# One trunk layer on one core: the attention loop in another order, and bias parts cut during the projection

## The chip, the cores and the metric

The kernel runs on one core of a Trainium2 chip. A core has a matrix engine (TensorE, PE in the profile), a vector engine (VectorE, DVE), an activation engine (ScalarE, ACT), a general engine (GpSimd, POOL) and a queue engine (SyncE, SP). Each takes its own instructions in order, and they meet at semaphores. The metric is the device time of one launch in microseconds, median of the runs; less is better.

## What is computed

One decoder layer over 512 tokens of width 1024, in float32. Only the attention and the first step of the expert part matter here:

```
sc = q k^T * scale + bias[bucket(distance)], masked
branch A (8 heads, 128-token window, sinks):  p = exp(sc - m) / (sum + exp(sink - m))
branch B (4 heads, two maps each, causal):    a = softmax(sc1) - lam * softmax(sc2)
o_a = p v;   o_b = rms_norm(a v) * (1 - lam_init)
y = sigmoid(gza) * (o_a @ w_out[:512]) + sigmoid(gzb) * (o_b @ w_out[512:])
...
gu = xb @ w_gate_up[e] + b_gate_up[e]       # 32 experts, each block
```

## The kernel before

**Stages.** The program runs one stage after another: the modulation rows, the projection with `w_in`, attention, the merge with router (`merge_*`), the experts, and the final sum. Matrices are held as a rounded high part and a low part and multiplied in three products. The weights `b_gate_up` (32 x 2048) are added to a sum of products by a matmul with a selection matrix; for that they are cut into three bfloat16 parts, 96 rows in all (`bparts`), in seven steps on DVE (`bias_parts(0)` to `bias_parts(6)`).

**Projection.** It has eight units of four output chunks; DVE also sums the rows of the modulation there (`ada`). For each half of a unit's weights ACT makes the high part (`split_high`, tile `whf`), DVE the low part (`split_low`, tile `wlf`), and PE multiplies. `whf` and `wlf` have two slots: PE works from one while the other is filled. ACT also copies each finished chunk out of PSUM (`evac_done`), in units 0 to 2 to `qk`, in units 3 to 7 to `nat`.

**Attention.** There are 24 units, six for each of four query tiles n of 128 tokens: two of branch A (four heads at a time), then four of branch B (one head with its two maps). For unit i:
- PE: `scores(i)` (L401 for A, L406 for B), `transposed(i)` (L420, L424: the weights p turned by matmuls with the identity), `values(i)` (L441, L449: the products with V), and once for each tile `outputs_transposed` (L457).
- DVE: `before(i)` (scale, bias, row maximum: L484 to L507) and `after(i)` (division by the sum, in B the difference of the maps: L517 to L529), once for each tile `sub_norm` (L553, L558), which between its two instructions waits for a power taken on POOL.
- ACT: `exps(i)` (L590, L593), `copies(i)` (L606, the turned weights from PSUM to SBUF, tile `pt`), then the output of A (L609, tile `ota`) or, after the last B head of a tile, the sums of squares (L615), and once for each tile L620.

Scores have two places in PSUM and four in SBUF (`s_sb`), `pt` has two. The turned weights have one place in PSUM. The order is written out by hand, with one loop on each engine: `AHEAD` is 3, so scores and exponentials run three units ahead of the products. `bias_parts` stand in DVE's loop at i = 8 to 14. POOL loads their source, `ball`, at the start of attention.

**Around it.** `merge_pe` begins with the output projection (L651) as soon as the last `outputs_transposed` is copied.

Of the kernel before, what the change touches and what calls it, by code (L numbers as in the profile page):

```python
# [96 lines left out]
def program(nc, ctx, x, c, rel_bias_table, w_ada, b_ada, g_mix_pre, g_mix_post, g_ffn_pre, g_ffn_post, w_in, w_out,  # L97
# [12 lines left out]
    h2_d = dram("h_ffn", (T, D), F32)  # L110
    slot_d = dram("slot_rows", (T * E, 2), I32)
# [23 lines left out]
    ball = at("ball", [96, 2 * D], F32, 52 * KB)  # L135
# [148 lines left out]
    def sem(name):  # L284
# [7 lines left out]
    oh_in, biasv_out, wide_out, toep_in, wo_in, ball_in, grow_in = map(  # L292
        sem, ("oh_in", "biasv_out", "wide_out", "toep_in", "wo_in", "ball_in", "grow_in"))
# [95 lines left out]

    def attention_pe(pe):  # L390
# [71 lines left out]
        for i in range(len(UNITS)):  # L462
            transposed(i)
            if i + AHEAD < len(UNITS):
                scores(i + AHEAD)
            values(i)
            if i >= 2 and UNITS[i - 2][0] == "B" and UNITS[i - 2][2] == H_B - 1:
                outputs_transposed(UNITS[i - 2][1])
        outputs_transposed(TC - 1)

    def attention_dve(dve):
# [60 lines left out]
        def bias_parts(n):  # L532


            if n == 0:
                dve.wait_ge(ball_in, 16 * 3)
                dve.wait_ge(latemod_ready, 3)
                nc.vector.tensor_scalar(ball[:, D:2 * D], ball[:, D:2 * D], 1.0, None, ALU.add).then_inc(bias_step, 1)
                dve.wait_ge(bias_step, 1)
                nc.vector.tensor_copy(bparts[:], ball[:]).then_inc(bias_step, 1)  # L540
                return

            cut, lo = ((False, 1), (False, 2), (True, 1), (True, 2), (False, 2), (True, 2))[n - 1]
            rows = slice(32 * lo, 32 * lo + 32)
            dve.wait_ge(bias_step, n + 1)
            if cut:
                nc.vector.tensor_copy(bparts[rows, :], ball[rows, :]).then_inc(bias_step, 1)
            else:
                nc.vector.tensor_tensor(ball[rows, :], ball[rows, :], bparts[rows, :], ALU.subtract).then_inc(bias_step, 1)

        def sub_norm(n):
            dve.wait_ge(osq_ready, H_B * (n + 1))
            nc.vector.tensor_scalar(sn[:, 1, :], sn[:, 0, :], 1.0 / (2 * DH), EPS_SUB, ALU.mult,  # L553
                                    ALU.add).then_inc(sn_ready, 1)
            dve.wait_ge(sn_ready, 2 * n + 2)
# [16 lines left out]
        for i in range(len(UNITS)):  # L572
# [4 lines left out]
            if i and UNITS[i - 1][0] == "B" and UNITS[i - 1][2] == H_B - 1:  # L577
                sub_norm(UNITS[i - 1][1])
            if 8 <= i < 8 + N_BIAS:
                bias_parts(i - 8)  # L580
# [1304 lines left out]
```

## Time and profile before

| | |
|---|---|
| median of 3 runs | 1775.54 us (1775.3 to 1778.35) |
| the profiled execution | 1777.53 us, its span 1775.7 us |
| PE busy | 1663.3 us, 94% of the span |
| DVE busy | 1377.4 us, 78% |
| ACT busy | 1097.6 us, 62% |
| mean granted clock of TensorE | 0.953 of full |

The span is what the profiler saw between the first and the last instruction; 1.8 us of the execution lie around it. The clock is a share of 2.4 GHz; in any stretch it is 1.0 or 0.5, and a number between is a mean. The shares are means over very different stages. Attention is the stretch from 249 to 369 us.

### The profile page before, as it was taken

What the parts mean: (1) busy time and instruction counts of PE and PEld (TensorE: products, weight loads), DVE (VectorE), ACT (ScalarE), POOL (GpSimd) and SP (SyncE); (2) the same over time, 40 slices, a digit from 0 to 9 for tenths busy, and PEclk for the clock granted to TensorE, in tenths of its full rate; (3) what the DMA queues carried; (4) which work ended last, traced back from release to release, by engine and by line L of the source; (5) the groups of instructions that cost most, each with busy time, mean ns of one, the idle gap of its engine ahead of it and who ended that gap; (6) DMA issues with size and microseconds to landing.
All of it is one profiled execution on the core that took longest, in us unless ns stands there. A gap on an engine that the chain in (4) does not pass through costs nothing.

```text
span 1775.7 us, 19642 instructions
## 1 busy us (share of the span) xinstructions
PE 1663.3 (94%) x7482; PEld 1299.8 (73%) x7482; DVE 1377.4 (78%) x1029; ACT 1097.6 (62%) x903; POOL 199.0 (11%) x154
## 2 busy tenths in 40 slices
PE   8999986688679999999999999999999999999994
PEld 3788864444368888888888888888888888888882
DVE  3544458825558888988898889988989898989894
ACT  2322235531447777777777777777777777777772
POOL 1200000021300001100110011001000100011112
PEclk9999997888579999999999999999999999999997
DMA  8765430022499999999999999999999999999964
GB/s 310 226 236 198 168 125 1 1 77 73 140 361 398 390 385 381 367 386 382 378 355 388 383 375 366 388 392 380 361 383 387 375 370 390 380 370 361 382 244 155
DMA packets 156502, 540.14 MB, mean 304 GB/s; under 512 B 13949, under 2 KB 15081, under 8 KB 156292
## 3 DMA queue, kind: packets, MB, share of 16 engines
q1 hardware_dynamic: 140880, 500.20, 74.0%
q0 software_dynamic: 13424, 34.47, 8.0%
q10 hardware_dynamic: 2100, 4.21, 0.7%
q8 instruction: 57, 0.93, 0.2%
q14 instruction: 41, 0.33, 0.0%
HBM read 522.54 MB, written 29.26 MB: 311 GB/s over the span
## 4 chain that ended last, share of the span: by engine, by line
PE 74%; DMA 2%; DVE 2%; ACT 1%; issue 1%; POOL 0%; POOLq 0%; SPq 0%; ACTq 0%; DVEq 0%
PE ps L1103 64%; PE ps L1077 4%; PE ps L651 4%; PE ps L1093 2%; PE ps L671 1%; DMA expert_sums<-yb,icur 0%; DMA xb<-h_ffn,stab 0%; DMA sums<-expert_sums 0%; PE ps L449 0%; PE ps L664 0%; ACT h2t L755 0%; DMA slot_rows<-rows,dest 0%; DVE y L831 0%; DVE yo L1364 0%; POOL slot_rows L931 0%
## 5 line engine op out<-in xcount | busy, mean ns | idle before, releaser
L1221 DVE TENSOR_TENSOR wl<-rawm,wh 128x2048 fp32r<-128x2048 f32 x420 | 946.7, 2286 | 147.6 <-ACT wh L1150 143.1
L1150 ACT ACTIVATE wh<-rawm 128x2048 fp32r<-128x2048 f32 x420 | 802.0, 1919 | 260.7 <-PE ps L1103 260.7
L1103 PE MATMUL ps<-wh,xh 128*128 128x512 f32 x1120 | 360.2, 403 | 3.5 <-DVE xl L1234 3.5
L1103 PE MATMUL ps<-wl,xh 128*128 128x512 f32 x1120 | 346.9, 391 | 0.0
L1103 PE MATMUL ps<-wh,xl 128*128 128x512 f32 x1120 | 346.2, 390 | 0.0
L1103 PEld LDWEIGHTS ps<-wh,xh 128*128 128x128 f32 x1120 | 211.3, 189 | 53.1 <-DVE xl L1234 4.9
L1103 PEld LDWEIGHTS ps<-wl,xh 128*128 128x128 f32 x1120 | 211.2, 189 | 44.8
L1103 PEld LDWEIGHTS ps<-wh,xl 128*128 128x128 f32 x1120 | 211.3, 189 | 44.5
L1103 PE MATMUL ps<-wh,ah 128*128 128x512 f32 x560 | 179.4, 401 | 2.5 <-DVE al L1238 2.5
L1103 PE MATMUL ps<-wl,ah 128*128 128x512 f32 x560 | 174.2, 392 | 0.0
L1103 PE MATMUL ps<-wh,al 128*128 128x512 f32 x560 | 173.1, 390 | 0.0
L1306 POOL DMA_INDIRECT expert_sums<-yb,stab x32 | 50.9, 1590 | 1009.0 <-ACT yb L1184 658.1
L1103 PEld LDWEIGHTS ps<-wh,al 128*128 128x128 f32 x560 | 105.6, 189 | 23.1
L1103 PEld LDWEIGHTS ps<-wl,ah 128*128 128x128 f32 x560 | 105.5, 188 | 22.7
L1103 PEld LDWEIGHTS ps<-wh,ah 128*128 128x128 f32 x560 | 100.3, 189 | 19.6 <-issue 3.0
L1745 DVE TENSOR_TENSOR wlf<-raw,whf 128x2048 fp32r<-128x2048 f32 (+1 forms) x18 | 39.1, 2173 | 90.1 <-ACT whf L1480 90.1
L1480 ACT ACTIVATE whf<-raw 128x2048 fp32r<-128x2048 f32 (+1 forms) x18 | 32.7, 1817 | 64.2 <-PE ps L1612 64.0
L1610 PE MATMUL ps<-whf,hh 128*128 128x512 f32 (+1 forms) x192 | 71.3, 372 | 0.0
L1612 PE MATMUL ps<-whf,hl 128*128 128x512 f32 (+1 forms) x192 | 71.1, 370 | 0.0
L1611 PE MATMUL ps<-wlf,hh 128*128 128x512 f32 (+1 forms) x192 | 71.0, 370 | 0.0
L1295 POOL DMA_INDIRECT xb<-h_ffn,stab x32 | 65.4, 2043 | 47.5 <-PE ps L1077 36.1
L1176 ACT ACTIVATE ah<-ps 128x1024 fp32r<-128x1024 f32 x35 | 35.9, 1026 | 55.3 <-PE ps L1103 55.3
(254 smaller groups left out, 1610.5 us busy)
## 6 DMA issues: line engine op xcount, KB each, us to landing
rawm<-in_w_gate_up SPq DMA_DIRECT2D x280, 1024.0 KB, 9.6
rawm<-in_w_down SPq DMA_DIRECT2D x140, 1024.0 KB, 7.8
raw<-in_w_ada SPq DMA_DIRECT2D x20, 1024.0 KB, 5.1
raw<-in_w_in SPq DMA_DIRECT2D x16, 1024.0 KB, 5.2
rawx<-in_w_ada SPq DMA_DIRECT2D x4, 1024.0 KB, 15.5
wo<-in_w_out SPq DMA_DIRECT2D x2, 2048.0 KB, 15.6
bias_vectors_repeated<-bias_vectors POOLq DMA_DIRECT2D x1, 2304.0 KB, 15.6
xs<-in_x ACTq DMA_DIRECT2D x1, 2048.0 KB, 12.9
```

The costliest lines, as they stand in the source:

```text
L651: ins = nc.tensor.matmul(ps[:, 2 * b + half, :], src[:, k, t * P:(t + 1) * P], wo[:, 4 * b + k, half * UN:(half + 1) * UN], start=(k == 0) ...
L1077: ins = nc.tensor.transpose(TURNED[:, k // 4, (k % 4) * P:(k % 4 + 1) * P], src[:, k * P:(k + 1) * P], ident[:])
L1103: ins = nc.tensor.matmul(banks[:, n, :], left[:, kk, :], right[:, k, n * UN:(n + 1) * UN], start=begins and kk == 0 and i == 0, stop=kk == ...
L1150: nc.scalar.activation(flat(wh[v % SPL][:]), flat(rawm[v][:]), ACT.Copy).then_inc(wh_done, 1)
L1176: nc.scalar.activation(flat(ah[:]), flat(TURNED), ACT.Copy).then_inc(ah_done, 1)
L1221: nc.vector.tensor_tensor(flat(wl[v][:]), flat(rawm[v][:]), flat(wh[v % SPL][:]), ALU.subtract).then_inc(wl_done, 1)
L1295: pool.indirect_dma_start(out=xb[:], out_offset=None, in_=h2_d, in_offset=bass.IndirectOffsetOnAxis(ap=column(0, p, gcur, p - (E - 1)), ax ...
L1306: pool.indirect_dma_start(out=sum_d, out_offset=bass.IndirectOffsetOnAxis(ap=column(1, p, done, p - (E - 1) if done is scur else 1), axis= ...
L1610: nc.tensor.matmul(dst, a_h, b_h, start=first, stop=False)
L1611: nc.tensor.matmul(dst, a_h, b_l, start=False, stop=False)
L1612: return nc.tensor.matmul(dst, a_l, b_h, start=False, stop=last)
L1745: nc.vector.tensor_tensor(wlf[:, m_slot, :, 0:n], raw[:, slot, :, 0:n], whf[:, m_slot, :, 0:n], ALU.subtract).then_inc(raw_used, 1)
```

## The change

In attention, `values` moves one unit back on PE, behind `transposed` of the next unit, and `scores(i + 3)` moves ahead of `transposed(i)`. On ACT `exps` runs two units ahead and no longer three, and the output copies become a step of their own, `outputs(i - 1)`, the last of each round. `sub_norm` is cut in two: `sub_norm_begun` one unit later than before, the rest two units later. `outputs_transposed` comes two rounds later on PE and three on ACT. `bias_parts` leaves attention for the rounds 0 to 2 of DVE's projection loop, which are therefore written out. Its tiles `ball` and `bmade` lie where `nat` will be, so ACT waits for them to be written to DRAM before its round 3; POOL reads them back to `bparts` in attention.

```diff
     def attention_pe(pe):
...
-        for i in range(len(UNITS)):
-            transposed(i)
+        for i in range(len(UNITS) + 1):
             if i + AHEAD < len(UNITS):
                 scores(i + AHEAD)
-            values(i)
-            if i >= 2 and UNITS[i - 2][0] == "B" and UNITS[i - 2][2] == H_B - 1:
-                outputs_transposed(UNITS[i - 2][1])
+            if i < len(UNITS):
+                transposed(i)
+            if i:
+                values(i - 1)
+            if tile_ended(i - 4) is not None:
+                outputs_transposed(tile_ended(i - 4))
...
     def attention_dve(dve):
...
-            if i and UNITS[i - 1][0] == "B" and UNITS[i - 1][2] == H_B - 1:
-                sub_norm(UNITS[i - 1][1])
-            if 8 <= i < 8 + N_BIAS:
-                bias_parts(i - 8)
+            if tile_ended(i - 2) is not None:
+                sub_norm_begun(tile_ended(i - 2))
+            if tile_ended(i - 3) is not None:
+                sub_norm(tile_ended(i - 3))
+        sub_norm_begun(TC - 1)
         sub_norm(TC - 1)
...
     def attention_act(act):
...
-        for i in range(AHEAD):
+        for i in range(AHEAD - 1):
             exps(i)
-        for i in range(len(UNITS)):
-            copies(i)
-            if i + AHEAD < len(UNITS):
-                exps(i + AHEAD)
-            if i >= 2 and UNITS[i - 2][0] == "B" and UNITS[i - 2][2] == H_B - 1:
-                outputs_transposed(UNITS[i - 2][1])
+        for i in range(len(UNITS) + 1):
+            if i < len(UNITS):
+                copies(i)
+            if i + AHEAD - 1 < len(UNITS):
+                exps(i + AHEAD - 1)
+            if i:
+                outputs(i - 1)
+            if tile_ended(i - 5) is not None:
+                outputs_transposed(tile_ended(i - 5))
...
     def merge_pe(pe):
         pe.wait_ge(wo_in, 32)
+        pe.wait_ge(bias_moved, 16 * 5)
...
         with act.Fori(0, N_T) as u:
             unit(u, to_qk)
+        act.wait_ge(bias_moved, 16 * 4)
         with act.Fori(N_T, N_W - 1) as u:
             unit(u, to_nat)
...
-        with dve.Fori(0, N_W - 1) as u:
+        for u, parts in enumerate(((0, 1), (2, 3, 4), (5, 6))):
+            unit(u)
+            for n in parts:
+                bias_parts(n)
+        with dve.Fori(N_T, N_W - 1) as u:
             unit(u)
...
         pool.wait_ge(hx_ready, TC)
         pool.dma_start(oh[:], oh_c).then_inc(oh_in, 16)
+        pool.wait_ge(hl_ready, KC)
+        for b in range(3):
+            pool.dma_start(ball[32 * b:32 * b + 32, :], b_gate_up[0]).then_inc(bias_moved, 16)
...
+        pool.wait_ge(bias_step, N_BIAS + 1)
+        pool.dma_start(bparts_d, bmade[:]).then_inc(bias_moved, 16)
...
-        for b in range(3):
-            pool.dma_start(ball[32 * b:32 * b + 32, :], b_gate_up[0]).then_inc(ball_in, 16)
+        pool.wait_ge(latemod_ready, 3)
+        pool.wait_ge(bias_moved, 16 * 4)
+        pool.dma_start(bparts[:], bparts_d).then_inc(bias_moved, 16)
```

How the rows stand on PE, at the A units of tile 2 (L420, L424 turn the weights, L406 makes scores, L441, L449 multiply with V); before:

```order
477 L424 MATMUL ps<-ident_143,s_sb3_58 128x128 x2
478 L406 MATMUL ps<-qk_107 128x384 x2
479 L449 MATMUL ps<-nat_109,pt_59 128x128 x2
480 L420 MATMUL ps<-ident_143,s_sb0_55 128x128 x8
481 L406 MATMUL ps<-qk_107 128x384 x2
482 L441 MATMUL ps<-pt_59,va_119 64x128 x8
```

The same place of the change, whose lines are some eight further on:

```order
477 L457 MATMUL ps<-nat_110,pt_59 128x128 x2
478 L414 MATMUL ps<-qk_108 128x384 x2
479 L428 MATMUL ps<-ident_144,s_sb0_55 128x128 x8
480 L457 MATMUL ps<-nat_110,pt_59 128x128 x2
481 L414 MATMUL ps<-qk_108 128x384 x2
482 L428 MATMUL ps<-ident_144,s_sb1_56 128x128 x8
483 L449 MATMUL ps<-pt_59,va_120 64x128 x8
```

Between the turning of a unit and its product with V now stand the scores and the turning of another unit. On ACT at the same place, before (L606 copies the turned weights, L590 the exponentials, L609 the output, L615 the squares):

```order
99 L606 ACTIVATE pt_59<-ps 128x256
100 L615 ACTIVATE osq_63,sn_171<-ps 128x128 x4
101 L590 ACTIVATE s_sb2_57,st_170<-s_sb2_57,st_170 128x384 x2
102 L606 ACTIVATE pt_59<-ps 128x1024
103 L609 ACTIVATE ota_60<-ps 128x2x128
104 L590 ACTIVATE s_sb3_58,st_170<-s_sb3_58,st_170 128x384 x2
```

And in the change (L600 is the copy, L584 the exponentials, L606 the output, L612 the squares):

```order
100 L600 ACTIVATE pt_59<-ps 128x1024
101 L584 ACTIVATE s_sb2_57,st_171<-s_sb2_57,st_171 128x384 x2
102 L612 ACTIVATE osq_63,sn_172<-ps 128x128 x4
103 L600 ACTIVATE pt_59<-ps 128x1024
104 L584 ACTIVATE s_sb3_58,st_171<-s_sb3_58,st_171 128x384 x2
105 L606 ACTIVATE ota_60<-ps 128x2x128
```

An output copy, which waits for a product with V, now stands behind the exponentials of its round and no longer between a copy and them.

## Rows read from the trace of the kernel before

**Rows 1.** Attention: length, busy of PE, weight loads, DVE, ACT, POOL; clock, DMA share, GB/s.

```profile
249.00:366.00 117.00, 76.39 (x429) 52.83 (x428) 93.16 (x193) 57.22 (x202) 3.07 (x3) 0.75 0.15 52
```

**Rows 2.** Instruction groups of DVE in attention, shapes apart: busy, mean ns, idle before.

```profile
L498 DVE SCALAR_TENSOR_TENSOR s_sb<-ps,toep 128x512 f32<-128x512 f32 x12 | 8.2, 686 | 4.2 <-PE ps L406 4.2
...
L549 DVE TENSOR_TENSOR ball<-ball,bparts 32x2048 f32<-32x2048 f32 x3 | 6.8, 2282 | 0.1
...
L547 DVE CAST bparts<-ball 32x2048 bf16<-32x2048 f32 x3 | 3.7, 1217 | 0.1
...
L558 DVE TENSOR_TENSOR on<-ps,sn 128x512 f32<-128x512 f32 x4 | 2.8, 692 | 4.5 <-POOL sn L1812 4.5
...
L498 DVE SCALAR_TENSOR_TENSOR s_sb<-ps,toep 128x256 f32<-128x256 f32 x4 | 1.7, 422 | 1.6 <-PE ps L406 1.6
...
L540 DVE CAST bparts<-ball 96x2048 bf16<-96x2048 f32 x1 | 1.2, 1223 | 0.0
...
L538 DVE TENSOR_SCALAR ball<-ball 96x1024 f32<-96x1024 f32 x1 | 0.7, 690 | 0.0
```

**Rows 3.** Timeline where a bias part runs: start, duration, instruction, idle before it.

```profile
293.67 2.28 DVE L549 TENSOR_TENSOR ball<-ball,bparts 32x2048 f32<-32x2048 f32 x1
293.74 0.51 ACT L590 ACTIVATE s_sb<-s_sb,st 128x256 f32<-128x256 f32 x1 [4.04 <-DVE st L492]
...
296.22 1.22 PE L449 MATMUL ps<-nat,pt 128*128 128x128 f32 x4 [2.86 <-ACT pt L606]
```

**Rows 4.** Timeline of two A units on DVE: one round from L484 to L498.

```profile
268.96 1.22 DVE L484 SCALAR_TENSOR_TENSOR s_sb<-ps,toep 128x1024 f32<-128x1024 f32 x1
...
273.29 0.68 DVE L498 SCALAR_TENSOR_TENSOR s_sb<-ps,toep 128x512 f32<-128x512 f32 x1
```

**Rows 5.** Timeline of PE in A units, first at the higher clock, then at the lower.

```profile
278.64 1.58 PE L441 MATMUL ps<-pt,va 128*64 128x128 f32 x16 [0.77 <-ACT pt L606]
...
280.15 1.10 PE L420 MATMUL ps<-ident,s_sb 128*128 128x128 f32 x8
...
287.33 1.14 PE L401 MATMUL ps<-ka,qk 64*128 64x256 f32 x8
...
291.28 2.09 PE L401 MATMUL ps<-ka,qk 64*128 64x256 f32 x8
...
303.94 1.97 PE L420 MATMUL ps<-ident,s_sb 128*128 128x128 f32 x8 [0.23 <-DVE s_sb L521]
...
308.36 2.88 PE L441 MATMUL ps<-pt,va 128*64 128x128 f32 x16 [0.87 <-ACT pt L606]
```

**Rows 6.** Timeline of the start and the end of attention and the first merge product.

```profile
249.82 0.69 DVE L484 SCALAR_TENSOR_TENSOR s_sb<-ps,toep 128x512 f32<-128x512 f32 x1 [1.24 <-PE ps L401]
...
355.95 0.75 DVE L529 SCALAR_TENSOR_TENSOR s_sb<-s_sb,st 128x512 f32<-128x512 f32 x1
...
358.88 2.07 PE L449 MATMUL ps<-nat,pt 128*128 128x128 f32 x8 [0.73 <-ACT pt L606]
...
362.55 2.08 PE L449 MATMUL ps<-nat,pt 128*128 128x128 f32 x8 [0.74 <-ACT pt L606]
...
369.21 9.03 PE L651 MATMUL ps<-wo,ota 128*128 128x512 f32 x16
```

**Rows 7.** Timeline of the projection around the start of its round 3, DVE's rows.

```profile
126.74 3.11 DVE L1724 SCALAR_TENSOR_TENSOR acc<-raw,cact,acc 128x512 f32 x4
135.91 2.29 DVE L1745 TENSOR_TENSOR wlf<-raw,whf 128x2048 fp32r<-128x2048 f32 x1 [6.06 <-ACT whf L1480]
```

**Rows 8.** The same place, ACT's rows.

```profile
133.97 1.91 ACT L1480 ACTIVATE whf<-raw 128x2048 fp32r<-128x2048 f32 x1
144.34 1.92 ACT L1480 ACTIVATE whf<-raw 128x2048 fp32r<-128x2048 f32 x1 [8.46 <-PE ps L1612]
```

**Rows 9.** DMA issues, KB each and median us to landing: one in the merge, one early.

```profile
expert_sums<-xb POOLq DMA_DIRECT2D x1, 512.0 KB, 2.9
...
grow<-in_g_ffn_pre POOLq DMA_DIRECT2D x1, 512.0 KB, 14.2
```

More of the change, by code:

```diff
@@ L110, in program @@
     h2_d = dram("h_ffn", (T, D), F32)
+    bparts_d = dram("gate_up_bias_parts", (96, 2 * D), BF16)
     slot_d = dram("slot_rows", (T * E, 2), I32)
@@ L134, in program @@
     osq = at("osq", [P, P], F32, 34 * KB)
-    ball = at("ball", [96, 2 * D], F32, 52 * KB)
+    ball = at("ball", [96, 2 * D], F32, 124 * KB)
+    bmade = at("bmade", [96, 2 * D], BF16, 132 * KB)
     wo = at("wo", [P, KC, D], F32, 64 * KB)
@@ L291, in program @@
     c_in, x_in, gpre_in, small_in, bada_in = map(sem, ("c_in", "x_in", "gpre_in", "small_in", "bada_in"))
-    oh_in, biasv_out, wide_out, toep_in, wo_in, ball_in, grow_in = map(
-        sem, ("oh_in", "biasv_out", "wide_out", "toep_in", "wo_in", "ball_in", "grow_in"))
+    oh_in, biasv_out, wide_out, toep_in, wo_in, bias_moved, grow_in = map(
+        sem, ("oh_in", "biasv_out", "wide_out", "toep_in", "wo_in", "bias_moved", "grow_in"))
     raw_in = [sem(f"raw_in{s}") for s in range(8)]
@@ L388, in scores_sb, with tile_ended @@
         return s_sb[i % IN_FLIGHT][:].rearrange("p (m k) -> p m k", m=2)[:, :, 0:keys(UNITS[i])[1] * P]
+    def tile_ended(i):
+        if 0 <= i < len(UNITS) and UNITS[i][0] == "B" and UNITS[i][2] == H_B - 1:
+            return UNITS[i][1]
+        return None
     def attention_pe(pe):
@@ L530, in after, with sub_norm_begun @@
                                            ALU.add).then_inc(p_ready, 1)
[L532 to L551, printed above, removed]
+        def sub_norm_begun(n):
             dve.wait_ge(osq_ready, H_B * (n + 1))
@@ L554, in sub_norm @@
                                     ALU.add).then_inc(sn_ready, 1)
+        def sub_norm(n):
             dve.wait_ge(sn_ready, 2 * n + 2)
@@ L606, in copies, with outputs @@
             nc.scalar.activation(dst, src, ACT.Copy).then_inc(pt_ready, 1)
+        def outputs(i):
+            kind, n, g = UNITS[i]
             act.wait_ge(o_ps, i + 1)
@@ L1788, in unit, with bias_parts @@
                 ada(4 + u, 1, 1, 3 + u, 13 + 4 * u, 12 + 4 * u)
-        with dve.Fori(0, N_W - 1) as u:
+        def bias_parts(n):
+            if n == 0:
+                dve.wait_ge(bias_moved, 16 * 3)
+                nc.vector.tensor_scalar(ball[:, D:2 * D], ball[:, D:2 * D], 1.0, None, ALU.add).then_inc(bias_step, 1)
+                dve.wait_ge(bias_step, 1)
+                nc.vector.tensor_copy(bmade[:], ball[:]).then_inc(bias_step, 1)
+                return
+            cut, lo = ((False, 1), (False, 2), (True, 1), (True, 2), (False, 2), (True, 2))[n - 1]
+            rows = slice(32 * lo, 32 * lo + 32)
+            dve.wait_ge(bias_step, n + 1)
+            if cut:
+                nc.vector.tensor_copy(bmade[rows, :], ball[rows, :]).then_inc(bias_step, 1)
+            else:
+                nc.vector.tensor_tensor(ball[rows, :], ball[rows, :], bmade[rows, :], ALU.subtract).then_inc(bias_step, 1)
+        for u, parts in enumerate(((0, 1), (2, 3, 4), (5, 6))):
[3 more added lines that the diff above has]
+        with dve.Fori(N_T, N_W - 1) as u:
             unit(u)
```

## Prediction

> **What bounds the kernel now.** The page's shares come first: PE is busy 94% of the span, so most of the time is matmuls. Those lie in the projection and the experts, and the change adds or removes no matmul. So I looked for the stretch in which PE is not dense and took the windows of attention: in 117 us PE is busy 76.4, DVE 93.2, ACT 57.2, at a mean granted clock of 0.75 [rows 1]. The clock has two levels there, 2.4 and 1.2 GHz, so it is at the lower one about half of the time. No engine is full, but DVE is the nearest to it. Nothing overlaps the whole of attention: the merge begins when its last copy is done, so what attention loses in length the program loses.
>
> The groups by line and shape then say what DVE does there [rows 2]. Of its work 6.8 + 3.7 + 1.2 + 0.7 = 12.4 us is on `ball`, the bias parts, which no unit of attention needs. It stands idle 4.2 us for scores of B units from PE (L406) and 4.5 us, four times 1.12, for the power on POOL between the halves of `sub_norm`. The two smaller score waits at the start, 1.6 us, belong to tile 0.
>
> The timeline shows how the engines hang together [rows 3]. While DVE subtracts a bias part for 2.28 us, ACT has just got the maxima for its exponentials after 4.04 us of waiting, and PE gets the copy of the turned weights, for which its product with V waited 2.86 us, only behind these exponentials. That is one loop through three engines: exponentials, copy, product with V, turning, scores, maxima, exponentials. `scores(i + 3)` stands behind `transposed(i)`, which stands behind `values(i - 1)`, which waits for a copy that ACT makes only after `exps(i + 1)`. DVE and PE take turns where they could overlap.
>
> **What the change removes, adds and moves.** From DVE's first row at 249.82 to the end of its last `after` at 355.95 + 0.75 = 356.70 it takes 106.9 us [rows 6].
>
> 1. *Bias parts out of attention*: 12.4 us off DVE's row there [rows 2]. On a DVE that is the pace all of it counts; on one that waits for the others anyway it counts less. I take the whole, since step 2 makes DVE the pace.
>
> 2. *The order*. `scores(i + 3)` now needs only `before(i + 1)` and the product two units back, and `values(i - 1)` needs a copy that has had the time of one turning and one set of scores. `exps(i + 2)` waits for maxima that DVE made a round earlier and so runs beside DVE's `after(i + 1)` and `before(i + 3)`. The score waits of 4.2 us go. With `sub_norm` cut by a round, three of the four power waits go, 3.4 us; the last one, behind unit 23, has nothing to hide it. The 1.6 us in tile 0 I leave: there ACT makes the third unit's exponentials only after the first copy. Sum 7.6 us [rows 2].
>
> DVE's stretch is then 106.9 - 12.4 - 7.6 = 86.9 us, if the others keep up. Do they? A round of two A units takes DVE 273.29 - 268.96 = 4.33 us [rows 4]. PE needs for one 1.14 + 1.10 + 1.58 = 3.8 us at the higher clock, but 2.09 + 1.97 + 2.88 = 6.9 us at the lower [rows 5]. So at the higher clock DVE is the pace, and at the lower PE, by 2.6 us for an A unit. There are six such units (tiles 1 to 3). ACT has 57.2 us of work in 86.9 and is not the pace [rows 1].
>
> 3. *Given back to the clock*. In the changed order PE does the same work in less time, so it pauses less, and I expect the lower level less often than in half of the time. I take a quarter: 1.5 A units at 2.6 make 3.9 us. The loss in the B units I take at 0.8 us each at the lower level (an estimate from the longest product with V, 2.07 us there [rows 6], half of it the excess, less the slack of DVE's shorter rounds); a quarter of twelve is 2.4, and that the slack of one round takes up. Bounds: 0 with no low stretch, 15.6 + 9.6 = 25.2 us with nothing else. I take 4, nearer the lower bound because a round at the higher clock leaves PE only 0.5 us free.
>
> 4. *The end*. From 356.70 to the first merge product at 369.21 pass 12.5 us. PE is two products behind DVE by then: they start at 358.88 and 362.55, 3.67 us apart, of which the product is 2.07 and the rest the turning and the copy between [rows 6]. In the changed order the copy of unit 23 runs beside the product of unit 22. Bounds: 0, if the last products stay at the lower clock and the extra lag eats the overlap; 2 x 1.6 for the gaps and 2 x 1.0 for the clock, 5.2 us. I take 2.5, the middle. The squares, the power and the last `sub_norm` stay.
>
> 5. *Bias parts in the projection*. DVE idles 6.06 us before each odd low part: its sums end at 126.74 + 3.11 = 129.85, the next starts at 135.91 [rows 7]. The three portions are 0.69 + 1.22 + 2.28 = 4.2, 2.28 + 2 x 1.22 = 4.7 and 2.28 + 1.22 = 3.5 us [rows 2], each below that. Cost 0; without that cover each would hold `wlf`, and 4 us behind it PE. Writing out three rounds of DVE's loop changes no work.
>
> 6. *ACT's new wait*, the one place where attention's gain could be paid back. The last part ends at 129.85 + 3.5 + about 0.1 = 133.5; POOL then writes 384 KB to DRAM, and ACT stands in front of its round 3, where it made `whf` at 133.97 [rows 8]. Behind ACT's wait stand that high part, then DVE's low part, then PE, which changes to this slot at 144.3: then it lets ACT have the other one [rows 8]. The late merge write of 512 KB landed after 2.9 us [rows 9]: ACT goes at 136.4, `wlf` is ready 1.91 + 2.29 us later at 140.6, 3.7 us before PE wants it. Cost 0. Other bound: the slowest early transfer took 14.2 us [rows 9]; then `wlf` is ready at 151.9 and PE waits 7.6 us. I take the first, since the early transfers ran beside full weight streams, while at 133 us nothing on PE's path is being fetched in a hurry. The evacuations of round 2 are all ahead of the wait.
>
> The Trainium skill speaks for a short wait too: by "DMA: Bandwidth & Descriptors", section on the anatomy of a DMA on the gpsimd path, such a transfer takes about 2.0 us plus bytes over 436 GB/s, here an estimated 2.9 us, so the sum would keep its zero. By the same rule the early 512 KB would have taken 3.2 us; the trace has 14.2 [rows 9], so it does not hold beside other traffic, and the range follows the row.
>
> 7. *Transfers*. The three loads of `ball`, 768 KB, leave a stretch in which DMA was 0.15 busy [rows 1] for an early one; on POOL's queue they pass the bias vectors, whose use begins at 249.82 [rows 6]. The read back of 384 KB to `bparts` comes early in attention, into that same empty share, and PE's added wait for it stands at the first merge product, some 100 us later. Cost 0.
>
> **Sum.** 12.4 + 7.6 - 4 + 2.5 = 18.5 us. The profiled execution took 1777.53 us, so 1759.0; it stood 2.0 above the median of the runs, and the sum moved to that median gives 1757.0 us.
>
> **Rivals.**
>
> *Only the bias parts count.* The loop of rows 3 closes in another place: product with V of an A unit waits for the output copy of the one before, which now stands behind exponentials. Then DVE goes on waiting, and of the gain 12.4 us remain: 1763. For it: ACT did wait for DVE 4 us at a time [rows 3]. Against it: ACT's own work fills two thirds of DVE's new stretch.
>
> *The clock stays low half of the time*, as now. Step 3 becomes half of 25.2, 12.6 us, step 4 about 1: the gain is 8.4, the time 1767. For it: 0.75 in [rows 1]. Against it: PE pauses less.
>
> *ACT held by the write*: 14.2 us instead of 2.9, PE waits 7.6 us, time 1764.6. For it the early rows, against it the 2.9 [rows 9].
>
> *Slower*: PE at 1.2 GHz through all of attention. It then is the pace in every unit after tile 0, gives back 25.2 us against the 20.0 of steps 1 and 2, with nothing from step 4: 5 us over, 1781. It decides from four fifths of the time at the lower level. For it: each A unit at that level costs 2.6 us [rows 4, 5]. Against it: it has the higher level for half of the time with a sparser PE.
>
> **How the numbers follow.** Forecast with its bounds (1750 to 1761) 0.60; only the bias parts 0.13; clock low for half 0.15; ACT held 0.05; slower 0.04; 0.03 for a gain lost to several of these, within no difference. A measurement of this kernel can tell some 0.2%, 3.6 us. The first four cases are faster by more: 0.93; within 0.03; slower 0.04. The range goes from 1750, where nothing is given back and the end brings 3, to 1767, where the half-low clock sits; outside lie half of that case, the two beyond it and a little below, under 0.2.
>
> **What would show it.** After the change DVE's stretch from the first L494 to the last `after` should be 85 to 93 us with no `ball` row and under 4 us of idle for scores; one wait of about 1.1 us for POOL in place of four, three of them gone; the granted clock of attention over 0.85; the three bias portions inside DVE's idle time in rounds 0 to 2 and PE without a wait between 66 and 246 us. ACT's high part of round 3 should start at 136 to 138 us. The prediction is wrong if PE's products with V still wait 1 to 3 us each, if attention's clock stays at 0.75, or if PE pauses near 144 us.

## The result, and the profile after

| | before | after |
|---|---|---|
| median | 1776.88 us (1775.3 to 1780.97, 5 runs) | 1753.69 us (1751.76 to 1755.93, 5 runs) |
| ratio | | 0.9868, 95% interval 0.9854 to 0.9883 |
| span of the profiled execution | 1775.7 us | 1750.0 us |
| mean granted clock of TensorE | 0.953 | 0.962 |

The change makes the kernel 23.2 us faster. The forecast was 1757.0, a gain of 18.5, in a range from 1750 to 1767.

Three windows after the change: the one of [rows 1], the one of attention as it now lies, and 4 us inside it; the columns are those of [rows 1]:

```profile
249.00:366.00 117.00, 88.24 (x483) 58.03 (x482) 87.15 (x196) 69.14 (x213) 12.39 (x18) 0.87 0.18 64
252.00:337.00 85.00, 59.96 (x391) 42.87 (x389) 79.71 (x185) 54.45 (x192) 3.58 (x4) 0.85 0.13 50
276.00:280.00 4.00, 4.00 (x17) 2.79 (x17) 3.81 (x10) 3.40 (x14) 0.00 (x0) 0.50 0.00 0
```

The first window no longer holds attention alone, since the merge begins inside it; the second is attention. DVE is busy 79.7 of 85 us there. The third is the one to remember: TensorE is at the lower of its two clocks and busy in all of the 4 us, and DVE is still busy in 3.81 of them.

DVE's groups with shapes apart, which answer to [rows 2]:

```profile
L508 DVE SCALAR_TENSOR_TENSOR s_sb<-ps,toep 128x512 f32<-128x512 f32 x12 | 8.2, 682 | 0.0
L494 DVE SCALAR_TENSOR_TENSOR s_sb<-ps,toep 128x1024 f32<-128x1024 f32 x6 | 7.3, 1217 | 0.0
L551 DVE TENSOR_TENSOR on<-ps,sn 128x512 f32<-128x512 f32 x4 | 2.8, 689 | 1.1 <-POOL sn L1835 1.1
...
L534 DVE RECIPROCAL st<-st 128x2 f32<-128x2 f32 x16 | 2.5, 158 | 0.9 <-ACT s_sb L584 0.9
L508 DVE SCALAR_TENSOR_TENSOR s_sb<-ps,toep 128x256 f32<-128x256 f32 x4 | 1.7, 416 | 0.0
```

The idle column of both L508 rows, which answer to L498 of before with 4.2 and 1.6 us, is 0.0. Of the four waits for POOL one is left, 1.1 us. No row of `ball` is there.

PE's groups over 252 to 337 us:

```profile
L457 PE MATMUL ps<-nat,pt 128*128 128x128 f32 x56 | 10.9, 334 | 5.1 <-DVE on L551 5.1
L428 PE MATMUL ps<-ident,s_sb 128*128 128x128 f32 x56 | 10.5, 344 | 11.8 <-DVE s_sb L531 11.7
...
L432 PE MATMUL ps<-ident,s_sb 128*128 128x128 f32 x35 | 7.8, 321 | 5.6 <-DVE s_sb L539 5.6
```

PE now waits for DVE (the divided weights and `on`) and not for ACT's copies. That is the picture of a pipeline with one pace setter: the waits point to it, and behind its first scores (1.24 us) it waits for others only 0.9 us in the whole stretch.

The timeline of the start and the end of attention, which answers to [rows 6]:

```profile
252.09 0.69 DVE L494 SCALAR_TENSOR_TENSOR s_sb<-ps,toep 128x512 f32<-128x512 f32 x1 [1.24 <-PE ps L409]
...
335.79 0.75 DVE L539 SCALAR_TENSOR_TENSOR s_sb<-s_sb,st 128x512 f32<-128x512 f32 x1
...
338.99 2.15 PE L457 MATMUL ps<-nat,pt 128*128 128x128 f32 x16
...
344.12 0.69 DVE L551 TENSOR_TENSOR on<-ps,sn 128x512 f32<-128x512 f32 x1 [1.12 <-POOL sn L1835]
...
345.77 1.91 PE L652 MATMUL ps<-wo,ota 128*128 128x512 f32 x2
```

DVE's stretch is 335.79 + 0.75 - 252.09 = 84.45 us instead of 356.70 - 249.82 = 106.88. The tail, from there to the first merge product, is 9.23 us instead of 12.5: the last two products with V (x16) follow each other without a gap and take 2.15 us together. The whole begins 2.27 us later than before, though. The sum is -22.43 - 3.28 + 2.27 = -23.4 us at the first merge product (369.21 and 345.77), and the rest of the 25.7 us between the spans, 2.3, comes behind it. Of that, 0.8 us is the first merge product itself: the next one starts 8.87 us behind it before and 8.11 us after, at a granted clock of 0.74 and 0.80 in the 8 us there. The other 1.5 us I did not trace. The profiled execution of the kernel after lies 1.9 us under its median, so that the medians differ by less than the spans.

**Where it begins late.** PE in the projection, and the `oh` and `ball` transfers (KB each, median us to landing):

```profile
67.07 0.80 PE L1641 MATMUL ps<-oh,tabx 33*8 33x384 f32 x2 [1.83 <-DMA oh<-const_buckets]
...
69.07 0.63 PE L1613 MATMUL ps<-hl,whf 128*128 128x512 f32 x1
```

```profile
ball<-in_b_gate_up POOLq DMA_DIRECT2D x3, 256.0 KB, 13.4
...
oh<-const_buckets POOLq DMA_DIRECT2D x1, 99.0 KB, 17.1
```

ACT's high parts of the projection, at either end of this piece:

```profile
42.01 1.04 ACT L1481 ACTIVATE whf<-raw 128x1024 fp32r<-128x1024 f32 x1
...
81.33 1.92 ACT L1481 ACTIVATE whf<-raw 128x2048 fp32r<-128x2048 f32 x1 [13.88 <-PE ps L1614]
```

The three early loads of `ball` are issued at 53.97 us, 4.1 us behind `oh` (99 KB), which PE needs at about 65 us. Before, `oh` landed after 14.4 us, now after 17.1, and PE stands still for 1.83 us. Behind the pause a product of this form is recorded with 0.63 us at first, and with 0.39 from 72.4 us on. From the first of these ACT rows to the last pass 39.3 us; in the kernel before they stand at 43.24 and 79.05, 35.8 us apart. So the early load costs 3.5 us, and of those 2.3 show in the start of attention, since this execution was 1.2 us ahead at 42 us.

**The new wait on ACT**, timeline of the projection at its round 3, which answers to [rows 7, 8]:

```profile
134.47 1.22 DVE L1805 CAST bmade<-ball 32x2048 bf16<-32x2048 f32 x1
...
139.54 1.92 ACT L1481 ACTIVATE whf<-raw 128x2048 fp32r<-128x2048 f32 x1 [3.20 <-DMA gate_up_bias_parts<-bmade]
141.49 2.29 DVE L1747 TENSOR_TENSOR wlf<-raw,whf 128x2048 fp32r<-128x2048 f32 x1 [5.80 <-ACT whf L1481]
...
146.61 1.92 ACT L1481 ACTIVATE whf<-raw 128x2048 fp32r<-128x2048 f32 x1 [5.16 <-PE ps L1614]
```

The write landed 3.3 us after its issue. `wlf` is ready at 141.49 + 2.29 = 143.78, and PE gives up the other slot at about 146.6: 2.8 us of slack, and PE has no wait there.

### The profile page after: what moved, and what is told of

It reads as the page before. It is cut to its first block, busy times and chain, and to the rows that moved or that the text cites. A ratio compares the mean times of both kernels' runs of the same rounds, so it can differ in the third digit from the quotient of the medians.

```text
span 1750.0 us, 19602 instructions
## 1 busy us (share of the span) xinstructions
PE 1649.9 (94%) x7482; PEld 1294.3 (74%) x7482; DVE 1376.4 (79%) x1029; ACT 1098.0 (63%) x903; POOL 200.4 (11%) x156
## 4 chain that ended last, share of the span: by engine, by line
PE 80%; issue 8%; DVE 5%; DMA 4%; ACT 2%; POOL 1%; SPq 0%; POOLq 0%; ACTq 0%; DVEq 0%
PE ps L1104 65%; PE ps L1078 4%; PE ps L652 3%; PE ps L1094 2%; PE ps L1612 1%; PE ps L1613 1%; PE ps L1614 1%; DMA raw<-in_w_ada 1%; DMA oh<-const_buckets 1%; DVE st L515 1%; PE ps L672 1%; PE ps L1559 1%; DMA grow<-in_g_ffn_post 0%; DMA expert_sums<-yb,icur 0%; DMA xb<-h_ffn,stab 0%
## 6 DMA issues: line engine op xcount, KB each, us to landing
wo<-in_w_out SPq DMA_DIRECT2D x2, 2048.0 KB, 12.4
xs<-in_x ACTq DMA_DIRECT2D x1, 2048.0 KB, 13.4
```

## The experiments

Twelve kernels ran, in three groups, each beside runs of the kernel before on its chip (medians 1779.64, 1778.34 and 1777.05 us; the ratio is taken against these). Start is DVE's first row of attention, stretch and tail are read from each trace as above (us).

| kernel | start | stretch | tail | median us | ratio, 95% interval |
|---|---|---|---|---|---|
| before | 249.82 | 106.9 | 12.5 | | |
| after | 252.09 | 84.45 | 9.2 | 1753.69 | 0.9868, 0.9854 to 0.9883 |
| e1_bias_only | 253.52 | 94.3 | 10.7 | 1768.77 | 0.9942, 0.9929 to 0.9956 |
| e2_order_only | 250.37 | 98.45 | 9.3 | 1763.64 | 0.9912, 0.9897 to 0.9927 |
| e3_late_load | 250.09 | 84.47 | 9.2 | 1749.89 | 0.9836, 0.9822 to 0.9851 |
| e8_write_thrice | 262.07 | 85.6 | 9.3 | 1762.65 | 0.9904, 0.9888 to 0.9920 |
| e4_pe_old | 254.77 | 104.6 | 11.9 | 1775.32 | 0.9978, 0.9968 to 0.9988 |
| e5_act_old | 255.47 | 105.75 | 9.9 | 1776.46 | 0.9995, 0.9984 to 1.0005 |
| e6_norm_whole | 251.73 | 88.6 | 7.2 | 1757.98 | 0.9885, 0.9868 to 0.9902 |
| e7_norm_early | 248.57 | 84.35 | 8.0 | 1749.09 | 0.9836, 0.9821 to 0.9851 |
| e9_dve_extra | 248.52 | 90.6 | 9.0 | 1758.07 | 0.9903, 0.9885 to 0.9921 |
| e10_act_extra | 251.43 | 85.8 | 8.8 | 1752.01 | 0.9862, 0.9844 to 0.9880 |
| e11_scores_back | 250.42 | 86.1 | 8.7 | 1753.34 | 0.9872, 0.9855 to 0.9888 |
| e12_exps_three | 250.39 | 85.7 | 7.1 | 1751.18 | 0.9855, 0.9839 to 0.9871 |

My theory was that attention, once the engines no longer take turns, runs at DVE's pace, and that the time saved is DVE's work and waits. The rival was that a loop through ACT and PE remains and that part of the saved work falls into waits.

### One half of the change alone

*e1_bias_only* is the kernel before with the bias parts moved and its old order:

```diff
-            if i:
-                values(i - 1)
+            values(i)
...
-            if i + AHEAD - 1 < len(UNITS):
-                exps(i + AHEAD - 1)
-            if i:
-                outputs(i - 1)
+            if i + AHEAD < len(UNITS):
+                exps(i + AHEAD)
```

> The change without its new attention order: the bias parts are cut in the projection, attention runs in the order of before. Theory A (in the old order DVE, ACT and PE wait for one another in a loop, so DVE's bias parts filled time that was partly waiting anyway): less than their 12.4 us comes off DVE's stretch, some 7 us, and DVE's idle time for scores grows; with about 2 us lost to the early load the time is 1772 us beside 1776.9 for before. Rival B (the bias parts are most of the gain, the order little): 12 us off the stretch, 1767 us.

*e2_order_only* has the new order with `bias_parts` back in attention:

```diff
             if tile_ended(i - 3) is not None:
                 sub_norm(tile_ended(i - 3))
+            if 8 <= i < 8 + N_BIAS:
+                bias_parts(i - 8)
```

> The new attention order alone: bias parts stay in attention, loaded where they were. Theory A (in the new order DVE sets the pace and never waits for scores): DVE's stretch is that of the change plus the whole 12.4 us of bias parts, 84.5 + 12.4 = 97 us, idle for scores under 1 us, and without the early load of ball PE does not wait for the one-hot table near 67 us: 1763 us. Rival B: the stretch stays above 102 us, 1769 us or more.

The groups of e1, DVE's scores and PE's product with V:

```profile
L457 PE MATMUL ps<-nat,pt 128*128 128x128 f32 x80 | 15.2, 328 | 22.4 <-ACT pt L593 22.4
...
L506 DVE SCALAR_TENSOR_TENSOR s_sb<-ps,toep 128x512 f32<-128x512 f32 x12 | 8.2, 687 | 4.7 <-PE ps L414 4.7
```

The bias parts take 12.6 us off the stretch (94.3), all of their 12.4, in the old order too. I had expected that part of them falls into waits there, and that was wrong: the waits for scores stayed nearly as they were, 6.3 us in all after 5.8. The order alone takes off 8.4 us (98.45; I expected 97). Together the two take off 22.4, which is 1.4 more than the sum of each alone, and 0.9 of this is one wait for scores in e2 that comes back below (e8). The gains add up, as on an engine that is the pace. PE's 22.4 us of waiting for copies in e1 is the old loop of [rows 3]; in the kernel after it is gone.

### The early load and the write

*e3_late_load* issues the loads of `ball` behind the bias vectors:

```diff
         pool.dma_start(oh[:], oh_c).then_inc(oh_in, 16)
-        pool.wait_ge(hl_ready, KC)
-        for b in range(3):
-            pool.dma_start(ball[32 * b:32 * b + 32, :], b_gate_up[0]).then_inc(bias_moved, 16)
         pool.wait_ge(rv_ready, 2)
         pool.dma_start(bias_d[0:H_A, :], rv[:, 0, :]).then_inc(biasv_out, 16)
         pool.dma_start(bias_d[H_A:H_A + H_B, :], rv[0:H_B, 1, :]).then_inc(biasv_out, 16)
+        pool.wait_ge(hl_ready, KC)
+        for b in range(3):
+            pool.dma_start(ball[32 * b:32 * b + 32, :], b_gate_up[0]).then_inc(bias_moved, 16)
```

> The change with the three loads of ball issued behind the bias vectors (near 70 us) and no longer right behind the last low part of h (near 54 us). Theory C (the early loads share the DMA engines with the one-hot table oh, which lands late, so PE waits 1.8 us near 67 us and runs at the lower clock for a few us behind it): that wait goes, 2 to 3 us less than the change, about 1751 us. Rival D (that wait is chance of this one execution): no difference to the change, 1753.7 us.

PE does not wait for `oh` any more, and attention's stretch is the same. The two rows of ACT that I used above:

```profile
43.51 1.04 ACT L1481 ACTIVATE whf<-raw 128x1024 fp32r<-128x1024 f32 x1
...
79.32 1.92 ACT L1481 ACTIVATE whf<-raw 128x2048 fp32r<-128x2048 f32 x1 [10.40 <-PE ps L1614]
```

They are 35.8 us apart, as in the kernel before: all of the 3.5 us are back. (e1, which has the early load, shows 39.2.) `oh` landed after 15.0 us in e3, 15.0 in e2 and 14.8 in e9, which load `ball` later, and after 17.0 in e1 and 17.6 in e8, which load it early, so this is not chance of one execution. The windows around 70 us, of the kernel after and then of e3:

```profile
68.00:74.00 6.00, 6.00 (x19) 4.43 (x18) 5.77 (x10) 0.00 (x0) 1.03 (x2) 0.72 0.99 267
```

```profile
68.00:74.00 6.00, 6.00 (x27) 4.98 (x27) 5.76 (x11) 0.92 (x1) 3.62 (x6) 1.00 0.68 180
```

In the same 6 us, both with PE busy throughout, the kernel after shows 19 records of matmuls at a clock of 0.72 and e3 27 at 1.00. So of the 3.5 us the pause itself is 1.8, and the other 1.7 lie behind it. By the ratios the gain is 0.0032 of 1777, 5.7 us, and their intervals leave room for the 3.5.

By the Trainium skill, "DMA: Bandwidth & Descriptors", section on the anatomy of a DMA on the gpsimd path, such a load takes 2.0 us plus bytes over 436 GB/s, an estimated 2.6 us for 256 KB. The three took 4.2 us (median) in e3, issued at 69.98 us, and 13.4 in the kernel after, issued at 53.97, where the DMA engines are busy throughout (1.04 of the window from 60 to 68 us): the rule is no bound there, and the row decides.

*e8_write_thrice* writes the bias parts three times, one after the other, and lets ACT wait for all of them:

```diff
-        act.wait_ge(bias_moved, 16 * 4)
+        act.wait_ge(bias_moved, 16 * 6)
...
         pool.dma_start(bparts_d, bmade[:]).then_inc(bias_moved, 16)
+        pool.wait_ge(bias_moved, 16 * 4)
+        pool.dma_start(bparts_d, bmade[:]).then_inc(bias_moved, 16)
+        pool.wait_ge(bias_moved, 16 * 5)
+        pool.dma_start(bparts_d, bmade[:]).then_inc(bias_moved, 16)
```

> The change with the write of the bias parts to DRAM done three times in a row, each waiting for the one before; ACT's wait ahead of its round 3 is for the third. It measures the slack of that wait. From the profile of the change (write 3.3 us, high part of round 3 at 139.54, low part ready at 143.78, PE changes slot near 146.6): slack 2.8 us, so two more writes at 3.3 to 3.8 us each make PE wait 4 to 5 us near 147 us, plus 1 to 3 us at the lower clock behind it: 1759 us. If ACT's wait had no such slack (PE already held by it), 7 us or more: 1761 us and up; if PE could go on without that low part, 1753.7 us.

```profile
150.27 3.71 ACT L1481 ACTIVATE whf<-raw 128x2048 fp32r<-128x2048 f32 x2 [10.36 <-DMA gate_up_bias_parts<-bmade]
```

```profile
154.56 0.50 PE L1612 MATMUL ps<-whf,hh 128*128 128x512 f32 x1 [4.50 <-DVE wlf L1747]
```

ACT goes 10.7 us later than in the kernel after, 3.6 of which this execution had lost before. The other 7.1 made PE wait 4.5, so the slack was 2.6 us, as the trace of the kernel after says (2.8). The chain that the prediction described is there; one write of 3.3 us does not reach its end. By the ratios e8 takes 6.4 us more than the kernel after, where I had expected 5.3: PE waits 4.5 us, and behind the pause the granted clock is 0.69 for 5.5 us. The median lies 3.7 us above my 1759, mostly because the kernel before, too, took 2.8 us more here (1779.64) than beside the result.

This run shows one thing more. Its attention is that of the kernel after, yet DVE's stretch is 85.6 us and not 84.45, because DVE waits once, for the first wide scores (tile 1):

```profile
277.47 1.23 DVE L494 SCALAR_TENSOR_TENSOR s_sb<-ps,toep 128x1024 f32<-128x1024 f32 x1 [1.15 <-PE ps L409]
```

PE's scores for it, in e8 and then in the kernel after:

```profile
275.25 2.09 PE L409 MATMUL ps<-ka,qk 64*128 64x256 f32 x8
```

```profile
264.63 1.14 PE L409 MATMUL ps<-ka,qk 64*128 64x256 f32 x8
```

The granted clock is 0.52 from 274 to 278 us in e8 and 1.00 at the same place, 264 to 268 us, in the kernel after. The wait stands at this place in e2 (0.9 us), e6 (1.0), e8 (1.15), e10 (1.1), e12 (1.4) and e11 (1.6), and not in the kernel after, e3, e7 and e9. In e2, e6 and e8 all that ran ahead of it in attention has the order of the kernel after. So the lower clock does cost DVE something in some executions, and a difference of about 1.1 us between two stretches says nothing about their orders.

### One engine in the old order

*e4_pe_old* is the kernel after with PE's rounds as before: turning, scores, product with V of the same unit. ACT and DVE keep the new order.

```diff
+            if i < len(UNITS):
+                transposed(i)
             if i + AHEAD < len(UNITS):
                 scores(i + AHEAD)
             if i < len(UNITS):
-                transposed(i)
-            if i:
-                values(i - 1)
+                values(i)
```

> The change with PE's loop in the order of before (turning, scores, product with V of the same unit); ACT and DVE as in the change. Theory A1 (the loop through three engines is broken by ACT's order alone, since the copy of a unit no longer stands behind exponentials that wait for scores of the same round): DVE's stretch 85 to 88 us beside 84.5 in the change, time up to 3 us above it. Theory A2 (the product with V one unit back is what breaks it): 92 us or more, 8 us above it.

*e5_act_old* has ACT's rounds as before: copy, output, exponentials three units ahead. PE and DVE keep the new order.

```diff
             if i < len(UNITS):
                 copies(i)
-            if i + AHEAD - 1 < len(UNITS):
-                exps(i + AHEAD - 1)
-            if i:
-                outputs(i - 1)
+                outputs(i)
+            if i + AHEAD < len(UNITS):
+                exps(i + AHEAD)
```

> The change with ACT's loop in the order of before (exponentials three units ahead, each output copy right behind the copy of the turned weights); PE and DVE as in the change. Theory A1: the exponentials wait behind an output copy, which waits for a product with V that PE now makes a unit later, so DVE waits for ACT: stretch 91 us, time 6 us above the change. Theory A2 (PE's order carries it): 85 to 88 us.

Both were far slower than any theory said: stretches of 104.6 and 105.75 us, 10 to 11 us longer than with the old order on all engines (e1, 94.3). Groups of e4:

```profile
L457 PE MATMUL ps<-nat,pt 128*128 128x128 f32 x80 | 19.5, 398 | 12.5 <-DVE on L551 9.3 <-ACT pt L600 3.1
...
L449 PE MATMUL ps<-pt,va 128*64 128x128 f32 x112 | 14.7, 348 | 7.7 <-ACT ota L606 7.3 <-ACT pt L600 0.3
...
L508 DVE SCALAR_TENSOR_TENSOR s_sb<-ps,toep 128x512 f32<-128x512 f32 x12 | 8.2, 686 | 6.6 <-PE ps L414 6.6
...
L494 DVE SCALAR_TENSOR_TENSOR s_sb<-ps,toep 128x1024 f32<-128x1024 f32 x6 | 7.3, 1220 | 6.9 <-PE ps L409 6.9
```

Groups of e5:

```profile
L432 PE MATMUL ps<-ident,s_sb 128*128 128x128 f32 x40 | 8.2, 306 | 18.5 <-ACT pt L600 18.4
...
L606 ACT ACTIVATE ota<-ps 128x256 f32<-128x256 f32 x8 | 3.1, 384 | 25.6 <-PE ps L449 25.6
...
L534 DVE RECIPROCAL st<-st 128x2 f32<-128x2 f32 x16 | 2.6, 164 | 21.6 <-ACT s_sb L584 21.5
```

In e5 ACT stands at the output of unit i (25.6 us in 8 waits) until PE has made a product that PE now makes one unit later, behind a turning that needs DVE; the exponentials for DVE stand behind that wait, and DVE waits 21.5 us for them. In e4 PE's product with V waits for two things that now come later than it does. That of an A unit waits for the output copy of the A unit before (7.3 us), which ACT makes last in its round, behind exponentials. That of a tile's first B unit waits for `on` of the tile before (9.3 us in three waits of 2.5 to 3.7), which DVE makes in the second half of `sub_norm`, two units later than in the kernel before. The next turning and scores stand behind the product, and DVE waits 6.6 + 6.9 us for scores, with 3.4 more at the narrow ones and 3.7 for exponentials. How much of e4's loss belongs to the copies and how much to the later `sub_norm` was not separated; no run has PE's old order with the old `sub_norm` and ACT's new order.

Which step of each engine's order does it? Two runs, made from e3, move the other step alone. *e11_scores_back* puts the scores behind the turning again and leaves `values(i - 1)`; it differs from e4 in attention only by the unit of `values`:

```diff
+            if i < len(UNITS):
+                transposed(i)
             if i + AHEAD < len(UNITS):
                 scores(i + AHEAD)
-            if i < len(UNITS):
-                transposed(i)
```

> The late-load kernel with the scores of unit i+3 again behind the turning of unit i on PE, the product with V staying one unit back. A, what closed the loop is that the product with V waits for its copy with the scores behind it: the product of the unit before is ready, so moving the scores costs little, stretch 84.5 to 86.5 us, time 1750 to 1752. B, it matters that the scores stand ahead of a turning that waits for DVE's division: the scores then come only after the division of unit i, which DVE makes a round earlier anyway, but the copies come earlier and the maxima later; DVE shows waits for scores of 3 us or more, stretch 88 to 92, time 1753 to 1757.

*e12_exps_three* makes the exponentials three units ahead and leaves `outputs(i - 1)` last; it differs from e5 in attention only by the place of the output copies:

```diff
-        for i in range(AHEAD - 1):
+        for i in range(AHEAD):
             exps(i)
...
-            if i + AHEAD - 1 < len(UNITS):
-                exps(i + AHEAD - 1)
+            if i + AHEAD < len(UNITS):
+                exps(i + AHEAD)
```

> The late-load kernel with ACT's exponentials again three units ahead, the output copies staying last in each round. A, exponentials of unit i+3 wait for the maxima that DVE makes in this same round, behind the division of unit i+1; the output copy of unit i-1 and the copy of unit i+1 stand behind this wait, and PE's turning of i+2 waits for the place in PSUM that the copy frees. ACT's wait then shows 1 to 2 us each round and the stretch grows by 5 to 10 us, time 1755 to 1760. B, the work ahead is deep enough: one unit more ahead costs nothing, stretch within 84 to 86 us, time 1750 to 1751.

A group of e12:

```profile
L432 PE MATMUL ps<-ident,s_sb 128*128 128x128 f32 x40 | 7.9, 298 | 8.2 <-ACT pt L600 8.2
```

The stretches are 86.1 and 85.7 us, against 104.6 and 105.75. So the product one unit back is worth 18.5 us where ACT's outputs stand last and `sub_norm` comes later, and the outputs last are worth 20 us where the product is one unit back. The place of the scores and the depth of the exponentials are worth 1.7 and 1.3 us at most, each with the other in the new order. These two are hardly more than the 1.1 us by which the same order varies; in both the wait of e8 is there, at 1.6 and 1.4 us, and e11 has 1.2 us more at the narrow scores of tile 0. No run has the pair alone, with scores and exponentials both in their old places. In e12 I had expected 5 to 10 us of loss from waits that do appear (PE waits 8.2 us at the B turnings for copies), but they lie on engines with slack, and DVE's stretch is 1.3 us longer.

### What paces the changed order

*e6_norm_whole* takes `sub_norm` in one piece again:

```diff
             if tile_ended(i - 2) is not None:
                 sub_norm_begun(tile_ended(i - 2))
-            if tile_ended(i - 3) is not None:
-                sub_norm(tile_ended(i - 3))
+                sub_norm(tile_ended(i - 2))
```

> The change with both halves of sub_norm in one round, the one where it now begins, so that DVE waits for the power on POOL between them. The prediction's step 2 counted three such waits of 1.12 us: stretch 84.5 + 3.4 = 87.8 us and the time 3.4 us above the change. The rival: PE gets the normalised outputs earlier, its product with V of the next tile no longer waits for them, and part of it comes back: 1 to 2 us above the change.

*e7_norm_early* is e3 with the second half of `sub_norm` ahead of `before(i + 3)`, so that PE gets `on` earlier:

```diff
+            if tile_ended(i - 3) is not None:
+                sub_norm(tile_ended(i - 3))
             if i + AHEAD < len(UNITS):
                 before(i + AHEAD)
             if tile_ended(i - 2) is not None:
                 sub_norm_begun(tile_ended(i - 2))
-            if tile_ended(i - 3) is not None:
-                sub_norm(tile_ended(i - 3))
```

> The late load of ball, and sub_norm's second half ahead of before(i + 3) in its round and no longer behind it. PE's waits for the normalised outputs (5.1 us in two rows in the change, and the lower clock behind them) go. Theory A (DVE is the pace): DVE's stretch stays at 84.5 us, the time within 1 us of the run with the late load alone, 1750 us. Rival (PE is part of the pace through its clock): 2 to 3 us less.

*e9_dve_extra* and *e10_act_extra* are e3 with a copy of 128x512 values in 20 rounds whose result nobody uses, on DVE or on ACT:

```diff
+            if 2 <= i < 22:
+                if i > 2:
+                    dve.wait_ge(fill_step, i - 2)
+                nc.vector.tensor_copy(fill[:], toep[:, 0:2, :].rearrange("p a k -> p (a k)")).then_inc(fill_step, 1)
```

> The late-load kernel (stretch of DVE in attention 84.5 us, 1749.9 us) with one copy of 128x512 float32 values more on DVE in each of the rounds 2 to 21 of attention, its result unused. Such a copy has no row of its own; a product of two operands of that size takes 0.68 us, a scaling 0.48, so 20 copies are about 20 x (0.35 to 0.7) = 7 to 14 us. A, DVE is the pace of the changed order: the stretch grows by the whole, to 92 to 98 us, and the time to 1757 to 1764. B, DVE and PE still take turns: a part of the copies lies in waits, the stretch grows by half of their sum or less.

> The late-load kernel with the same copy on ACT in place of DVE, behind the exponentials of the rounds 2 to 21: a copy of that size takes ACT about 0.60 us, so 20 are 12 us, more work than the run before puts on DVE. A, DVE is the pace and ACT has slack: ACT is busy 55 of the 87 us, so the stretch stays within 84.5 to 87 us and the time within 1750 to 1753. B, ACT lies on the loop: the stretch grows by 6 to 12 us.

Group and timeline of e9, group of e10:

```profile
L575 DVE COPY fill<-toep 128x512 f32<-128x512 f32 x20 | 8.4, 420 | 0.0
...
337.23 0.42 DVE L575 COPY fill<-toep 128x512 f32<-128x512 f32 x1
337.57 0.16 DVE L536 RECIPROCAL st<-st 128x2 f32<-128x2 f32 x1
```

```profile
L632 ACT ACTIVATE fill<-toep 128x512 f32<-128x512 f32 x20 | 12.3, 616 | 0.0
```

A copy is recorded with 0.42 us, and the next instruction starts 0.34 us after the copy's start, so 20 of them take 6.8 us of DVE's row. The stretch grew by 6.1, nine tenths. On ACT 12.3 us of work, nearly twice as much, lengthened it by 1.3, of which 1.1 is the wait that e8 shows. The stretch of e9 lies under my 92 to 98 only because the copy was cheaper than its bounds. With e6, where three waits of 1.1 us for POOL came back on DVE and the stretch grew by 4.2 (expected 3.4; 1.0 is the wait that e8 shows, and it stands ahead of the first `sub_norm`), and e7, where PE got its operand earlier and the stretch did not move (84.35), this shows that DVE is the pace. e7's order starts the merge product 1.2 us sooner behind the stretch than e3's (tail 8.0 and 9.2 us); its time, 1749.09 us at the same ratio of 0.9836, cannot be told from e3's. These two are the fastest kernels here.

## Why the prediction was right, point by point

**What bounds attention, and step 1 (bias parts, 12.4).** Right: 12.6 in e1. Its reason, "I take the whole, since step 2 makes DVE the pace", was not needed: e1 does not have step 2, and there too the whole counts.

**Step 2 (the order, 7.6).** Right in size: in the stretch the score waits of 4.2 and three power waits of 3.4 are gone. The 1.6 us of tile 0, which I left standing, went as well. The reasons were right only in part. The text gave first place to scores that need only `before(i + 1)`, and to exponentials beside DVE's work. These are worth 1.7 and 1.3 us at most (e11, e12). What opens the loop is the product one unit back together with the output copy behind the exponentials, and in the new order taking back either one costs some 20 us. The text has the product between the two others, and the output copy stands in it only as the start of the rival *only the bias parts count*. It did not see that the product must also come behind the later `sub_norm` (9.3 us of waiting for `on` in e4).

**Step 3 (given back to the clock, 4).** The term that was mis-sized, and most of the 4.7 us by which the gain exceeds the forecast. The clock itself was as forecast: 0.85 over the 85 us, which with levels of 1.0 and 0.5 is the lower one for 0.30 of the time, where I had said a quarter. But in this execution it cost nothing that DVE shows. 12.4 + 5.8 + 3.4 = 21.6 us of the 22.4 are DVE's work and waits that went, and the idle before L494 and L508 is 0.0, even though PE ran at the lower clock and was busy in all of 276 to 280 us. In e8, with the same order in attention, it cost 1.15 us at one place, so the term is 0 to about 1.1 us where I had 4. I had compared one A unit of PE (6.9 us) with one round of DVE (4.33) and counted the difference as lost; the scores stand three units ahead, and a unit that PE does late is caught up from that stock. That the stock is the reason is argued, no run shortened it.

**Step 4 (the end, 2.5).** 3.3 us, within its bounds. 1.8 of it appears in e1 too, whose order is the old one; there it cannot come from the order. The clock goes with the tail: e1's last two products take 1.16 us each where before they took 2.07 and 2.08, and with the new order the tail is 9.2 us in the kernel after at a granted clock of 0.81 and 7.1 in e12 at 0.99. How the 3.3 us divide between clock and order is open.

**Step 5 (bias parts in the projection, 0).** Right: the three portions lie in DVE's idle time. DVE still waits 2.25 and 1.35 us for ACT's high part before the first two low parts behind them (at 95.02 and 116.53). Before the third it waits 5.80 us (at 141.49), since ACT itself waits for the write there.

**Step 6 (ACT's wait, 0).** Right. The write took 3.3 us for my 2.9, ACT went at 139.54 and not at 136.4 (the last part ended at 135.69, not at 133.5), mostly because the projection was late by then, and 2.8 us of slack were left for my 3.7. e8 shows the chain behind it.

**Step 7 (transfers, 0).** Here a step failed. I wrote that the loads of `ball` "leave a stretch in which DMA was 0.15 busy [rows 1] for an early one" and looked only at what they pass on POOL's queue. What they disturbed was a transfer already on its way: `oh` of 99 KB landed 2.7 us later (2.1 later than in e3), PE waited 1.83 us, and with the clock behind it 3.5 us were lost, all of which e3 wins back.

So 23.4 us at the first merge product are 18.5 of the sum, plus 4.0 not lost to the clock, 1.6 in tile 0, 0.8 at the end and 0.8 in small waits that I can't assign, less 2.3 for the later start; what follows adds 2.3. Two misses of opposite sign made the total look better than its parts: that the time lies in the range is partly luck.

The lower end of the range was summed wrongly. "Nothing is given back and the end brings 3" gives 12.4 + 7.6 + 3 = 23 us off 1775.54, which is 1752.5; 1750 takes step 4 at its upper bound of 5.2.

**Signs.** The stretch of 84.45 us lies just under the 85 to 93 of the text; no `ball` row, no idle for scores, one wait for POOL, as said. The clock is 0.85 to 0.87. "PE without a wait between 66 and 246 us" was wrong by the wait for `oh`, and ACT's high part of round 3 at 139.54 lies behind its 136 to 138. The rivals: what remained of e1 is *only the bias parts count* (a gain of 10 us there), and the full kernel is beyond it. The slower case, PE at 1.2 GHz as the pace, did not come; but slower kernels than the forecast were near, by another way than that one: with PE or ACT left in the old order nearly nothing of the gain remains (ratios 0.9978 and 0.9995), even with the bias parts out of attention.

## What to carry to other kernels

When several engines run in order over the same units, the wait that the trace shows is the symptom of a loop, and the loop opens only when all its ends move: shift a product by a unit only together with the steps that free the place of its result. Once the pace setter waits for nobody, price a change by its row, and charge it for the slower clock of an engine that works ahead of it only where that engine's lead runs out (0 to 1.1 us here, where 4 were forecast). Before reading a small difference between two traces as the effect of an edit, look at what the same code differs by (1.1 us of stretch here). A transfer that is moved earlier must be weighed against what is on its way at that time, not only against its own queue.

## What was not expected of the hardware

A pause of 1.83 us of TensorE in the dense projection was followed by a stretch of 6 us with a granted clock of 0.72, and cost nearly as much again as it lasted (3.5 us in all). Three loads of 256 KB beside the weight streams, with the DMA engines busy 0.99 to 1.04 of the windows there, took 13.4 us (median) and 4.2 when issued 16 us later. One of 99 KB, issued 4.1 us ahead of them, landed after 17.1 us, against 15.0 with the later loads and 14.4 before. The same attention program ran with a mean granted clock of 0.85 over 85 us in the kernel after and 0.81 in e8, and only at the lower of these did VectorE wait for scores.
